# Three fill tiles per recurrence chunk, 116 fill units per attention head, and the second expert table without a loop

## The chip, the cores and the metric

The kernel runs on one core of a Trainium2 chip. The metric is device time in microseconds (us) of one execution, the median of three runs. A core has five engines that run side by side and wait for each other on semaphores: TensorE (PE; its weight loads are shown apart as PEld), VectorE (DVE), ScalarE (ACT), GpSimd (POOL) and SyncE (SP). SP, ACT and POOL also start DMA transfers. Each engine takes its instructions strictly in the order in which they were written.

## The reference

One step of a streaming encoder layer for 512 prompt and 32 sample positions (544 columns, width 2048), all in 32-bit floats:

```
h = rmsnorm(x); qkv|z|b|a|dq|dk|dv|gate_a|gate_b = split(h @ w_in)
o_a = gated_delta_rule(conv(qkv), ...)        # blocks of 64 positions, a state carried from block to block
o_b = (softmax1 - lam * softmax2) @ V          # 8 heads, block-causal
x += (sigmoid(gate_a)*(o_a @ w_a) + sigmoid(gate_b)*(o_b @ w_b)) @ w_out
x += cross_attend(rmsnorm(x), memory)
x += sum over 8x16 chosen experts of gate * gelu(xb . u[e]) * v[e]     # tables u, v: 16384 x 2048
y  = rmsnorm(x)
```

The expert layer is computed for 416 of the 544 columns by running all 16384 experts (gates of the experts not chosen are zero), and for the other 128 columns (the tail) by fetching the chosen rows of u and v.

## The kernel before

All large products are made from halves: a weight tile of 128x2048 is loaded into one of four ring slots, ACT rounds it (round_w, round_e: 128x2048), DVE subtracts the rounded part from the tile (split_w, split_e: 128x2048), and PE multiplies hi*hi, hi*lo and lo*hi. PE may begin tile n when the split of n is done, ACT may round tile n when PE has finished tile n-2, and SP may load it when PE has finished tile n-4. So every tile passes through ACT and DVE, in their order of instructions, while PE works on the tile before.

**Fill.** 56 tiles (projections of h for q, k, v and the two gates of the attention branch) are not computed in a stage of their own. They are cut in 32 units each, three matmuls of 272 columns per unit, and the function fill (L861) puts units into PE's stream between the small steps of two stages that are chains of PE, ACT and DVE: 9 chunks of the recurrence (128 units, four tiles, in each) and 8 heads of the attention (80 units in each). The tables GDN_FILL and ATT_FILL give the number of units ahead of each wait: d_a units ahead of the wait for DVE's d_a, a_x ahead of ACT's a_x, and so on. On ACT, serve (L1390) evicts each half tile (16 units), sends it out by DMA and after a full tile rounds the next but one. On DVE, split_w stands at fixed places of a chunk; in the attention, split_tiles (L1855) puts the split of the tile that begins at unit 32k behind the part q of the head in whose stretch unit 32k - 12 lies. In part 0 of each head but the first, head_norm (L1847) of the head before stands ahead of that split.

**Second table.** 128 tiles of v, 48 matmuls of 416 columns each, in 17 segments: 4 tiles, 15 times 8 tiles, 4 tiles. PE runs segments 1 to 14 as a hardware loop of seven passes of 16 tiles (L1263), the others are written out. At a segment's end DVE adds the eight PSUM banks into Y (sums). Per tile DVE also adds one fetched expert row block into the tail (tail_add, 128x2048). Once in 8 tiles two sets of coefficients (four experts' rows each) are loaded (load_quad on SP), multiplied (coefficients, on DVE), rounded (round_c, on ACT) and split (split_c, on DVE); the set for tiles 8B+2 and 8B+3 is needed two tiles after the first.

**Final norm.** ACT squares Y, PE sums the squares over 2048 rows with 64 matmuls against a matrix of ones, ACT takes the root, DVE the reciprocal, and 16 products give the result, which SP sends out in four parts.

Of the kernel before, what the change touches and what calls it, by code (L numbers as in the profile page):

```python
# [72 lines left out]

F_GDN = 4 * (NCH + 1)
W_BEFORE = W_MERGE + T_PQ - T_MERGE
# [32 lines left out]
def program(nc, t):  # L108
    with ExitStack() as ctx:
# [310 lines left out]
        def hi_of(n):  # L420
            return w_first[n % 2] if n < T_FILL else f_hi[n % 2] if n <= T_FILL + F_GDN else w_hi[n % 2]

# [93 lines left out]
        pick_v = [view(arena, KD * NT + b * D, 1, D)[0][:, 0, :] for b in range(4)]  # L516
        Y = H[:, :, :]
        Z = M
        e_in = [sem(f"e_in{b}") for b in range(R)]
# [27 lines left out]
        def _(sp):  # L547
# [26 lines left out]
            for tile in range(T_FILL + R, T_MERGE + R):  # L574
                c = (tile - R - T_FILL) // 4 + 1
                if (tile - R - T_FILL) % 4 == 0 and 2 <= c <= NCH:
# [201 lines left out]
        def _(pe):  # L778
# [457 lines left out]

            def pair_tiles(m0, begins, ends, seg, reg=None):

                for p in range(4):
                    n = E_V + m0 + p  # L1240
                    first, last = begins and p == 0, ends and p == 3
                    pe.wait_ge(w_split, upto(W_BEFORE + n + 1, reg, 16))
                    if m0 % 8 == 0 and p % 2 == 0:
                        pe.wait_ge(c_split, upto(m0 // 4 + p // 2 + 1, reg, 4))
                    for d in range(8):
                        if first:
                            pe.wait_ge(y_free, upto(8 * seg + d + 1, reg, 16))
# [30 lines left out]
            pe.wait_ge(y_free, 8 * N_BLOCKS + 16)  # L1278
            norm_pe(pe, "final", Z)


        @block.scalar
        def _(act):
# [366 lines left out]
            act.wait_ge(x_done, 3)  # L1650
            norm_act(act, "final", Y, Z)


        @block.vector
        def _(dve):
# [111 lines left out]
            def gdn_block(c, dyn):  # L1767
# [7 lines left out]
                if c:  # L1775
                    split_w(T_FILL + 4 * c + 1)
                dve.wait_ge(s["p_g"], one)
# [29 lines left out]
                    .then_inc(s["d_r"], 1)  # L1807
                split_w(T_FILL + 4 * c + 2)
                for lv in range(1, LEVELS):
# [6 lines left out]
                    if lv == 2:  # L1816
                        split_w(T_FILL + 4 * c + 3)
                dve.wait_ge(s["p_ks"], one)
# [379 lines left out]
            def sums(seg):  # L2198
                for d in range(8):
                    dst = Y[:, 8 * (seg % 2) + d, 0:ND]  # L2200
                    dve.wait_ge(y_full, 8 * seg + d + 1)
                    nc.vector.tensor_tensor(dst, dst, psum[:, d, 0:ND], ALU.add).then_inc(y_free, 1)

            for B in range(N_BLOCKS):
                more = B < N_BLOCKS - 1
                for half in range(2):
                    for p in range(4):
# [7 lines left out]
                        if m == 3:  # L2215
                            dve.wait_ge(x_moved, 48)
                        if m % 8 == 3 or m == 8 * N_BLOCKS - 1:
# [8 lines left out]
            dve.drain().then_inc(x_done, 1)  # L2226
            dve.wait_ge(root_ready, 5)
            nc.vector.reciprocal(root, root)
            dve.drain()
# [149 lines left out]
```

## Time and profile before

| | |
|---|---|
| three runs | 5408.36, 5415.87, 5424.44 us (median 5415.87) |
| profiled execution | 5427.89 us, its span from first to last instruction 5426.3 us |
| PE busy | 5176.1 us (95%), 36030 matmuls |
| DVE busy | 3011.2 us (55%) |
| ACT busy | 1616.1 us (30%) |
| POOL busy | 574.0 us (11%) |
| mean granted TensorE clock | 0.978 of full speed |

Times inside the profile count from the span's start. The recurrence lies at 660 to 1285, the attention at 1300 to 1706, the second table at 4091 to 5380 and the final norm at 5380 to 5426. A busy PE is not a PE at full pace: the duration of a matmul overlaps that of the next, and its pace is the distance from start to start. The granted clock of a stretch is 1.00 where TensorE had its 2.4 GHz all through, and lower where it ran some of the time at 1.2 GHz.

### The profile page before, as it was taken

How to read it: one execution, taken by the hardware profiler on the slowest of the kernel's cores; microseconds unless marked ns; L12 is line 12 of the kernel's file. 1: busy time of each engine (PE TensorE's matmuls, PEld its weight loads, DVE VectorE, ACT ScalarE, POOL GpSimd, SP SyncE). 2: the span in 40 equal slices, each digit the busy share in tenths (PEclk: the TensorE clock that was granted, in tenths of full speed). 3: DMA queues.
4: the chain of work that ended last, by engine and by line, in shares of the span. 5: the costliest groups of instructions: out<-in, count | busy, mean ns of one | idle time of the engine just before them, and what ended most of it. 6: DMA issues, size and time to landing. Idle time of an engine off the chain costs nothing.

```text
span 5426.3 us, 83831 instructions
## 1 busy us (share of the span) xinstructions
PE 5176.1 (95%) x36030; PEld 4981.6 (92%) x36030; DVE 3011.2 (55%) x4155; ACT 1616.1 (30%) x1765; POOL 574.0 (11%) x534
## 2 busy tenths in 40 slices
PE   7999999998888999999899999999999989999997
PEld 6999999997788999979899999999999989988897
DVE  5455544434555333222799788875545655655565
ACT  4434322223443222131222343432222222222222
POOL 0000000000000000000000122222211111111110
PEclk9999999999999999999999999999999999999999
DMA  6422332223223322222322588887767677777673
GB/s 229 153 101 99 109 92 83 90 88 104 88 99 121 131 94 83 89 86 86 125 102 102 209 313 306 311 309 278 277 227 288 245 254 248 245 256 245 239 270 138
DMA packets 257568, 951.58 MB, mean 175 GB/s; under 512 B 46464, under 2 KB 130560, under 8 KB 179456
## 3 DMA queue, kind: packets, MB, share of 16 engines
q1 hardware_dynamic: 181792, 552.11, 29.9%
q0 software_dynamic: 59360, 379.63, 18.4%
q10 hardware_dynamic: 16128, 15.60, 0.8%
q8 instruction: 228, 3.74, 0.3%
q14 instruction: 60, 0.49, 0.0%
HBM read 855.84 MB, written 91.43 MB: 175 GB/s over the span
## 4 chain that ended last, share of the span: by engine, by line
PE 78%; DVE 10%; issue 4%; DMA 2%; DVEq 2%; ACT 2%; PEld 1%; PEldq 0%; ACTq 0%; SPq 0%; POOL 0%; POOLq 0%
PE psum L1177 18%; PE psum L1252 16%; PE psum L1067 11%; PE psum L873 10%; PE psum L845 7%; PE psum L1084 4%; DVE e_lo L1984 2%; PE psum L821 2%; PE psum L1216 2%; PE psum L806 1%; DMA arena<-gates 1%; PEld psum L1252 1%; DVEq L2196 1%; DVE tmp L1883 1%; DMA ring<-in_v 1%
## 5 line engine op out<-in xcount | busy, mean ns | idle before, releaser
L1984 DVE TENSOR_TENSOR e_lo<-ring,e_hi 128x2048 fp32r<-128x2048 f32 x270 | 618.7, 2292 | 507.9 <-ACT e_hi L1495 491.6
L1495 ACT ACTIVATE e_hi<-ring 128x2048 fp32r<-128x2048 f32 x270 | 517.3, 1916 | 1009.1 <-PE psum L1252 851.2
L1252 PE MATMUL psum<-c_hi,e_hi 128*128 128x416 f32 x2048 | 733.9, 358 | 71.4 <-issue 36.2
L1252 PE MATMUL psum<-c_lo,e_hi 128*128 128x416 f32 x2048 | 727.4, 355 | 17.8 <-issue 17.8
L1252 PE MATMUL psum<-c_hi,e_lo 128*128 128x416 f32 x2048 | 731.5, 357 | 0.0
L1177 PE MATMUL psum<-h_hi,e_hi 128*128 128x416 f32 x2032 | 718.5, 354 | 5.5 <-DVE e_lo L1984 5.5
L1177 PE MATMUL psum<-h_hi,e_lo 128*128 128x416 f32 x2048 | 721.8, 352 | 0.0
L1177 PE MATMUL psum<-h_lo,e_hi 128*128 128x416 f32 x2032 | 710.4, 350 | 0.0
L873 PE MATMUL psum<-p_hi,e_lo 128*128 128x272 f32 x1792 | 525.0, 293 | 0.0
L1252 PEld LDWEIGHTS psum<-c_hi,e_hi 128*128 128x128 f32 x2048 | 392.4, 192 | 87.7 <-issue 63.7
L1252 PEld LDWEIGHTS psum<-c_lo,e_hi 128*128 128x128 f32 x2048 | 392.8, 192 | 27.2 <-issue 21.1
L1252 PEld LDWEIGHTS psum<-c_hi,e_lo 128*128 128x128 f32 x2048 | 392.2, 191 | 3.7
L1177 PEld LDWEIGHTS psum<-h_hi,e_hi 128*128 128x128 f32 x2032 | 381.5, 188 | 11.2 <-DVE e_lo L1984 7.7
L1177 PEld LDWEIGHTS psum<-h_lo,e_hi 128*128 128x128 f32 x2032 | 382.1, 188 | 5.4
L1177 PEld LDWEIGHTS psum<-h_hi,e_lo 128*128 128x128 f32 x2048 | 384.0, 188 | 3.1
L873 PE MATMUL psum<-p_hi,f_hi 128*128 128x272 f32 x1184 | 360.2, 304 | 0.7 <-ACT arena L1383 0.7
L873 PEld LDWEIGHTS psum<-p_hi,e_lo 128*128 128x128 f32 x1792 | 346.5, 193 | 0.0
L873 PE MATMUL psum<-p_lo,f_hi 128*128 128x272 f32 x1184 | 341.4, 288 | 0.0
L773 POOL DMA_INDIRECT arena<-in_v,eidx x128 | 221.7, 1732 | 1033.8 <-DVEq L2196 1007.4
L1580 ACT ACTIVATE tmp<-psum 128x416 f32<-128x416 f32 x128 | 66.3, 518 | 818.0 <-PE psum L1177 818.0
L2194 DVE SCALAR_TENSOR_TENSOR arena<-arena 128x2048 f32<-128x2048 f32 x127 | 297.9, 2345 | 0.0
L1297 ACT ACTIVATE w_hi<-ring 128x2048 fp32r<-128x2048 f32 x83 | 158.6, 1911 | 317.4 <-PE psum L1067 164.4
(433 smaller groups left out, 10227.1 us busy)
## 6 DMA issues: line engine op xcount, KB each, us to landing
ring<-in_weights SPq DMA_DIRECT2D x200, 1024.0 KB, 4.8
ring<-in_uT SPq DMA_DIRECT2D x128, 1024.0 KB, 5.1
ring<-in_v SPq DMA_DIRECT2D x128, 1024.0 KB, 7.0
hid<-tmp POOLq DMA_DIRECT2D x128, 208.0 KB, 6.2
gates<-arena POOLq DMA_DIRECT2D x13, 2048.0 KB, 10.0
arena<-hid SPq DMA_DIRECT2D x32, 832.0 KB, 10.5
arena<-gates SPq DMA_DIRECT2D x32, 832.0 KB, 13.9
gate_in<-tmp ACTq DMA_DIRECT2D x64, 136.0 KB, 2.9
```

Source lines behind the costliest of these rows:

```text
L773: pool.indirect_dma_start(pick_v[k % 4], None, experts, bass.IndirectOffsetOnAxis(eidx[:, k:k + 1], 0))\
L821: mm = nc.tensor.matmul(psum[:, 2 * (n % 2), 0:MEM], a, b[:, k, :], start=(k == 0 and j == 0), stop=(k == KD - 1 and j == 2))
L845: mm = nc.tensor.matmul(acc[j % 2][:, b, :], a, x[:, k, b * HN:(b + 1) * HN], start=(k == 0 and n == 0), stop=(k == KD - 1 and n == 2))
L873: mm = nc.tensor.matmul(psum[:, b, 0:HN], a, x[:, k, tok], start=(k == 0 and n == 0), stop=(k == KD - 1 and n == 2))
L1067: mm = nc.tensor.matmul(acc[j % 2][:, b, :], w, x[:, k, b * HN:(b + 1) * HN], start=(k == 0 and n == 0), stop=(k == KD - 1 and n == 2))
L1084: mm = nc.tensor.matmul(dst[:, b, :], a, x[:, k, b * HN:(b + 1) * HN], start=(k == 0 and n == 0), stop=(k == HEADS - 1 and n == 2))
L1177: mm = nc.tensor.matmul(psum[:, 2 + r % 2, 0:ND], w, h[:, c, 0:ND], start=(c == 0 and i == 0), stop=(c == KD - 1 and i == 2))
L1252: mm = nc.tensor.matmul(psum[:, d, 0:ND], w, c[p // 2][:, 2 * (p % 2) + r, :], start=(first and r == 0 and j == 0), stop=(last and r == 1 ...
L1297: nc.scalar.activation(hi_of(n), ring[:, tile % R, :], ACT.Copy).then_inc(w_rounded, 1)
L1495: nc.scalar.activation(hi_slot(n, reg), e_raw[n % R], ACT.Copy).then_inc(w_rounded, 1)
L1984: nc.vector.tensor_tensor(e_lo[n % R], e_raw[n % R], as_f32(hi_slot(n, reg)), ALU.subtract)\
L2194: add = nc.vector.scalar_tensor_tensor(out=ytok, in0=pick_v[k % 4], scalar=coef_t[:, k:k + 1], in1=ytok, op0=ALU.mult, op1=ALU.add)
```

## The change

Four things are edited. A chunk of the recurrence takes three tiles of the fill (96 units) and a head of the attention 116 units, with new tables of where the units stand; the fourth split_w of a chunk goes, and the others follow the new tile numbers. PE's loop over the second table is written out. In the second table, ACT rounds a set of coefficients ahead of the tile round that it stood behind, DVE makes both sets one tile later, and tail_add of the first two rows moves behind the splits of tiles 2 and 3. The final norm is taken apart: the 416 columns are squared row by row as they come out of the last two segments and added on DVE, so that one matmul is left for them, and the 128 tail columns follow with 16 matmuls of 128 columns.

```diff
-GDN_FILL = {"c_qb": 8, "c_kv": 16, "d_gu": 4, "d_a": 26, "d_r": (8, 7, 7, 7, 7), "a_x": 4, "d_rr": 9,
-            "a_vn": 5, "a_o": 4}
-ATT_FILL = {"vt": 6, "a": (10, 9, 11, 13, 13), "aT": (2, 2, 2, 5, 2), "obs": 5}
-GDN_UNITS, ATT_UNITS = 128, 80
+GDN_FILL = {"c_qb": 8, "c_kv": 20, "d_gu": 4, "d_a": 16, "d_r": (5, 5, 5, 5, 5), "a_x": 2, "d_rr": 6,
+            "a_vn": 4, "a_o": 3}
+ATT_FILL = {"vt": 12, "a": (14, 12, 14, 16, 17), "aT": (8, 4, 3, 6, 4), "obs": 6}
+F_CHUNK = 3
+GDN_UNITS, ATT_UNITS = F_CHUNK * F_TILE, 116
...
-                split_w(T_FILL + 4 * c + 4)
...
-            with pe.Fori(0, N_BLOCKS // 2 - 1) as i:
-                pair_tiles(4, True, False, 1, i)
-                pair_tiles(8, False, True, 1, i)
-                pair_tiles(12, True, False, 2, i)
-                pair_tiles(16, False, True, 2, i)
-            pair_tiles(8 * N_BLOCKS - 12, True, False, N_BLOCKS - 1)
-            pair_tiles(8 * N_BLOCKS - 8, False, True, N_BLOCKS - 1)
+            for seg in range(1, N_BLOCKS):
+                pair_tiles(8 * seg - 4, True, False, seg)
+                pair_tiles(8 * seg, False, True, seg)
...
-            norm_pe(pe, "final", Z)
+            pe.wait_ge(sq_added, SQ_DENSE + KD - 1)
+            nc.tensor.matmul(psum[:, 4, 0:ND], ones, dense_sq, start=True, stop=True).then_inc(ss_ready, 1)
+            for c in range(4):
+                pe.wait_ge(sq_tile, 3 * KD + c + 1)
+                for k in range(4):
+                    mm = nc.tensor.matmul(psum[:, 5, 0:TAIL], ones, tail_sq[:, 4 * c + k, :],
+                                          start=(c == 0 and k == 0), stop=(c == 3 and k == 3))
...
+            def dense_square(n):
+                act.wait_ge(x_tile, 2 * KD + n + 1)
+                if n >= 3:
+                    act.wait_ge(sq_added, SQ_DENSE + max(n - 3, 1))
+                nc.scalar.activation(dense_rows[n % 3], Y[:, last_order(n), 0:ND], ACT.Square).then_inc(sq_tile, 1)
...
-                    if n < E_END:
-                        round_e(n)
                     if B < N_BLOCKS - 1 and p == 6:
                         round_c(2 * B + 2)
                     if B and p == 0:
                         round_c(2 * B + 1)
+                    if n < E_END:
+                        round_e(n)
...
+                    if seg >= N_BLOCKS - 1:
+                        dve.drain().then_inc(x_tile, 1)
+                    if seg == N_BLOCKS and d:
+                        dense_add(KD // 2 + d - 1)
...
-                        tail_add(m)
-                        if more and (m % 8 == 3 or m % 8 == 4):
-                            coefficients(2 * B + 2 + (m % 8) // 4)
+                        if m < 8 * N_BLOCKS - 1:
+                            for k in tail_rows(m):
+                                tail_add(k)
+                        if more and (m % 8 == 4 or m % 8 == 5):
+                            coefficients(2 * B + 2 + m % 8 - 4)
```

On PE, at the end of a pass over 16 tiles of the second table, stood before (L1263 is the loop, c_hi, c_lo the coefficients' halves, e_hi, e_lo the tile's):

```order
L1252 MATMUL psum<-c_hi1_74,e_hi1_72 128x416
L1252 MATMUL psum<-c_lo1_76,e_hi1_72 128x416
L1252 MATMUL psum<-c_hi1_74,e_lo3_58 128x416
L1263 REGISTER_ALU
L1263 COMPARE_AND_BRANCH
```

and in the changed kernel at the same point, the next tile's first matmul directly behind:

```order
L1265 MATMUL psum<-c_lo1_76,e_hi1_72 128x416
L1265 MATMUL psum<-c_hi1_74,e_lo3_58 128x416
L1265 MATMUL psum<-c_hi0_73,e_hi0_71 128x416 [waits y_free,w_split]
L1265 MATMUL psum<-c_lo0_75,e_hi0_71 128x416
L1265 MATMUL psum<-c_hi0_73,e_lo0_55 128x416
```

The branch and its register step are gone; the matmuls and their order are the same.

On ACT, inside a block of 8 tiles of the second table, stood before (e_hi is a tile's rounded half, c_hi a set of coefficients):

```order
L1495 ACTIVATE e_hi1_72<-ring 128x2048 [waits e_end,e_in3]
L1495 ACTIVATE e_hi0_71<-ring 128x2048 [waits e_end,e_in0]
L1628 ACTIVATE c_hi0_73<-arena 128x1664 [waits e_end,c_ready]
L1495 ACTIVATE e_hi1_72<-ring 128x2048 [waits e_end,e_in1]
L1495 ACTIVATE e_hi0_71<-ring 128x2048 [waits e_end,e_in2]
L1628 ACTIVATE c_hi1_74<-arena 128x1664 [waits e_end,c_ready]
L1495 ACTIVATE e_hi1_72<-ring 128x2048 [waits e_end,e_in3]
```

and in the changed kernel:

```order
L1511 ACTIVATE e_hi1_72<-ring 128x2048 [waits e_end,e_in3]
L1644 ACTIVATE c_hi0_73<-arena 128x1664 [waits e_end,c_ready]
L1511 ACTIVATE e_hi0_71<-ring 128x2048 [waits e_end,e_in0]
L1511 ACTIVATE e_hi1_72<-ring 128x2048 [waits e_end,e_in1]
L1644 ACTIVATE c_hi1_74<-arena 128x1664 [waits e_end,c_ready]
L1511 ACTIVATE e_hi0_71<-ring 128x2048 [waits e_end,e_in2]
```

Each c_hi has moved ahead of one tile's round, whose wait is for one tile more of PE.

On DVE, in part 0 of the attention's third head (from the last product of the part to the next part's scores; L1850 and L1852 are head_norm), stood before:

```order
L1891 SCALAR_TENSOR_TENSOR H<-H,tmp 128x128
L1850 RECIPROCAL tmp<-tmp 128x544 [waits att_rt]
L1852 SCALAR_TENSOR_TENSOR arena<-tmp,lamb 128x544
L1872 SCALAR_TENSOR_TENSOR H<-H,const,psum 128x256 [waits att_s]
L1883 TENSOR_REDUCE tmp<-H 128x1
```

and in the changed kernel:

```order
L1926 SCALAR_TENSOR_TENSOR H<-H,tmp 128x128
L1885 RECIPROCAL tmp<-tmp 128x544 [waits att_rt]
L1887 SCALAR_TENSOR_TENSOR arena<-tmp,lamb 128x544
L1706 TENSOR_TENSOR e_lo3_58<-ring,w_hi1_60 128x2048 [waits w_rounded]
L1907 SCALAR_TENSOR_TENSOR H<-H,const,psum 128x256 [waits att_s]
```

A split now stands behind head_norm; before, part 0 of no head had one.

## Rows read from the trace of the kernel before

**Rows 1.** Busy time by stretch (start:end us, engines, granted clock, DMA share, GB/s).

```profile
4139.00:4288.00 149.00, 145.85 (x769) 143.18 (x768) 98.01 (x61) 36.59 (x20) 28.24 (x16) 1.00 0.78 272
4288.00:4454.00 166.00, 151.55 (x770) 147.60 (x768) 96.06 (x56) 36.57 (x20) 26.58 (x16) 0.95 0.70 244
4620.00:4781.00 161.00, 150.06 (x771) 146.06 (x769) 96.05 (x56) 36.59 (x20) 28.24 (x16) 0.97 0.72 252
946.00:1017.00 71.00, 71.00 (x856) 65.67 (x854) 29.96 (x43) 20.10 (x29) 0.00 (x0) 1.00 0.29 87
1300.00:1706.00 406.00, 364.61 (x2544) 328.67 (x2544) 211.78 (x370) 163.66 (x338) 19.09 (x36) 0.94 0.26 90
```

**Rows 2.** Waits, second table and final norm: total us, times, longest.

```profile
PE psum L1252 <- issue: 54.0, 21, 5.9
PE psum L1252 <- DVE e_lo L1984: 33.9, 20, 6.8
```

**Rows 3.** Waits, the loop's first pass alone (4139 to 4288).

```profile
PE psum L1252 <- issue: 0.3, 1, 0.3
```

**Rows 4.** Timeline of PE at the second jump back (start, duration, idle before).

```profile
4459.59 0.71 PE L1252 MATMUL psum<-c_hi,e_hi 128*128 128x416 f32 x1 [5.35 <-issue]
```

**Rows 5.** Timeline of DVE, second table, third pass.

```profile
4514.39 1.89 DVE L2171 TENSOR_TENSOR c_lo<-arena,c_hi 128x1664 fp32r<-128x1664 f32 x1 [8.26 <-ACT c_hi L1628]
4518.66 2.29 DVE L1984 TENSOR_TENSOR e_lo<-ring,e_hi 128x2048 fp32r<-128x2048 f32 x1
...
4557.53 1.89 DVE L2166 TENSOR_TENSOR arena<-arena 128x1664 f32<-128x1664 f32 x1 [8.62 <-DMA arena<-gates]
```

**Rows 6.** Timeline of DVE and ACT, beginning of the second table.

```profile
4114.25 1.29 DVE L2192 TENSOR_SCALAR arena<-arena 128x2048 f32<-128x2048 f32 x1 [17.32 <-DMA arena<-in_v,eidx]
4133.41 1.92 ACT L1495 ACTIVATE e_hi<-ring 128x2048 fp32r<-128x2048 f32 x1 [20.24 <-DMA ring<-in_v]
```

**Rows 7.** Chain that ended last (start, us, what): final norm, and fill in a chunk.

```profile
5389.64 16.61 PE psum L266 x64
946.12 10.01 PE psum L873 x78
```

**Rows 8.** Timeline of DVE, final norm.

```profile
5380.21 0.59 DVE L2202 TENSOR_TENSOR H<-H,psum 128x416 f32<-128x416 f32 x1 [0.55 <-PE psum L1252]
5407.01 3.55 DVE L2228 RECIPROCAL tmp<-tmp 128x544 f32<-128x544 f32 x1 [19.60 <-ACT tmp L200]
```

**Rows 9.** Timeline of DVE in one chunk of the recurrence.

```profile
946.21 0.16 DVE L1778 COPY tmp<-psum 128x4 f32<-128x4 f32 x1 [2.98 <-PE psum L922]
949.10 0.43 DVE L1787 TENSOR_TENSOR tmp<-tmp,const 128x256 f32<-128x256 f32 x1 [1.40 <-ACT tmp L1421]
950.93 0.42 DVE L1794 TENSOR_TENSOR tmp<-tmp,const 128x256 f32<-128x256 f32 x1
952.82 0.68 DVE L1800 TENSOR_TENSOR tmp<-H,tmp 128x512 f32<-128x512 f32 x1
956.79 0.42 DVE L1803 TENSOR_TENSOR tmp<-const,psum 128x256 f32<-128x256 f32 x1 [3.29 <-PE psum L929]
957.62 0.42 DVE L1806 TENSOR_TENSOR tmp<-tmp,const 128x256 f32<-128x256 f32 x1
```

**Rows 10.** Timeline of ACT at a chunk's end.

```profile
1001.17 0.40 ACT L1401 ACTIVATE tmp<-psum 128x272 f32<-128x272 f32 x1 [1.46 <-PE psum L873]
1003.98 1.28 ACT L1437 ACT_TABLE_LOAD   x1
```

**Rows 11.** Timeline of DVE in one head of the attention.

```profile
1452.51 0.35 DVE L1872 SCALAR_TENSOR_TENSOR H<-H,const,psum 128x128 f32<-128x128 f32 x1 [7.22 <-PE psum L1013]
1455.07 0.35 DVE L1891 SCALAR_TENSOR_TENSOR H<-H,tmp 128x128 f32<-128x128 f32 x1
1458.96 0.78 DVE L1852 SCALAR_TENSOR_TENSOR arena<-tmp,lamb 128x544 f32<-128x544 f32 x1
1472.65 2.28 DVE L1670 TENSOR_TENSOR e_lo<-ring,w_hi 128x2048 fp32r<-128x2048 f32 x1
```

More of the change, by code:

```diff
@@ L72 @@
 W_MERGE = T_MERGE
-F_GDN = 4 * (NCH + 1)
+F_GDN = F_CHUNK * (NCH + 1)
 W_BEFORE = W_MERGE + T_PQ - T_MERGE
@@ L517, in program, with last_order @@
         Y = H[:, :, :]
+        dense_rows = [view(arena, 3 * D + b * ND, 1, ND)[0][:, 0, :] for b in range(3)]
+        dense_sq = view(arena, 3 * D + 3 * ND, 1, ND)[0][:, 0, :]
+        tail_sq, e = view(arena, BIG + 4 * CQ, KD, TAIL)
+        assert 4 * ND <= D and e <= BIG + OAB_N
+        SQ_DENSE = 1 + 2 * (KD - 2)
+        flat_root = root.rearrange("p a b -> p (a b)")
+        def last_order(n):
+            return (n + KD // 2) % KD
         Z = M
@@ L574, in _ @@
             for tile in range(T_FILL + R, T_MERGE + R):
-                c = (tile - R - T_FILL) // 4 + 1
-                if (tile - R - T_FILL) % 4 == 0 and 2 <= c <= NCH:
+                c = (tile - R - T_FILL) // F_CHUNK + 1
+                if (tile - R - T_FILL) % F_CHUNK == 0 and 2 <= c <= NCH:
                     load_chunk(c)
@@ L1235, in _, with pair_tiles @@
             pe.sem_inc(y_free, 8)
-            def pair_tiles(m0, begins, ends, seg, reg=None):
+            def pair_tiles(m0, begins, ends, seg):
                 for p in range(4):
@@ L1278, in _ @@
             pe.wait_ge(y_free, 8 * N_BLOCKS + 16)
-            norm_pe(pe, "final", Z)
+            pe.wait_ge(sq_added, SQ_DENSE + KD - 1)
[5 more added lines that the diff above has]
+                                          start=(c == 0 and k == 0), stop=(c == 3 and k == 3))
+            mm.then_inc(ss_ready, 1)
         @block.scalar
@@ L1649, in _ @@
                         round_c(2 * B + 1)
-            act.wait_ge(x_done, 3)
-            norm_act(act, "final", Y, Z)
+                    if n < E_END:
+                        round_e(n)
+                    if n >= E_END - 2 and n < E_END:
+                        for k in range(4):
+                            dense_square(4 * (n - E_END + 2) + k)
+            for n in range(KD // 2, KD):
+                dense_square(n)
+            for c in range(4):
+                act.wait_ge(x_tile, 3 * KD + c + 1)
+                nc.scalar.activation(tail_sq[:, 4 * c:4 * c + 4, :], Y[:, 4 * c:4 * c + 4, ND:NT], ACT.Square)\
+                    .then_inc(sq_tile, 1)
+                if c == 1:
+                    act.wait_ge(ss_ready, SUMS["final"])
+                    nc.scalar.activation(flat_root[:, 0:ND], psum[:, 4, 0:ND], ACT.Sqrt, bias=eps, scale=1.0 / D)\
+                        .then_inc(root_ready, 1)
+            act.wait_ge(ss_ready, SUMS["final"] + 1)
+            nc.scalar.activation(flat_root[:, ND:NT], psum[:, 5, 0:TAIL], ACT.Sqrt, bias=eps, scale=1.0 / D)\
+                .then_inc(root_ready, 1)
         @block.vector
@@ L1775, in gdn_block @@
                 if c:
-                    split_w(T_FILL + 4 * c + 1)
+                    split_w(T_FILL + F_CHUNK * c + 1)
                 dve.wait_ge(s["p_g"], one)
@@ L1807, in gdn_block @@
                     .then_inc(s["d_r"], 1)
-                split_w(T_FILL + 4 * c + 2)
+                split_w(T_FILL + F_CHUNK * c + 2)
                 for lv in range(1, LEVELS):
@@ L1816, in gdn_block @@
                     if lv == 2:
-                        split_w(T_FILL + 4 * c + 3)
+                        split_w(T_FILL + F_CHUNK * c + 3)
                 dve.wait_ge(s["p_ks"], one)
@@ L2202, in sums, with dense_add, tail_rows @@
                     nc.vector.tensor_tensor(dst, dst, psum[:, d, 0:ND], ALU.add).then_inc(y_free, 1)
+                    if seg >= N_BLOCKS - 1:
+                        dve.drain().then_inc(x_tile, 1)
+                    if seg == N_BLOCKS and d:
+                        dense_add(KD // 2 + d - 1)
+                if seg == N_BLOCKS:
+                    dense_add(KD - 1)
+            def dense_add(n):
+                dve.wait_ge(sq_tile, 2 * KD + n + 1)
+                nc.vector.tensor_tensor(dense_sq, dense_rows[0] if n == 1 else dense_sq, dense_rows[n % 3], ALU.add)
+                dve.drain().then_inc(sq_added, 1)
+            def tail_rows(m):
+                if m < 2:
+                    return range(0)
+                return range(m - 2 + min(m - 2, 2), m - 1 + min(m - 1, 2))
             for B in range(N_BLOCKS):
@@ L2216, in _ @@
                             dve.wait_ge(x_moved, 48)
+                        if m >= 8 * N_BLOCKS - 3:
+                            for n in range(*((1, 4), (4, 7), (7, 8))[m - 8 * N_BLOCKS + 3]):
+                                dense_add(n)
+                        if m == 8 * N_BLOCKS - 1:
+                            tail_add(m)
                         if m % 8 == 3 or m == 8 * N_BLOCKS - 1:
                             sums((m + 1) // 8)
-                        tail_add(m)
-                        if more and (m % 8 == 3 or m % 8 == 4):
-                            coefficients(2 * B + 2 + (m % 8) // 4)
+                        if m < 8 * N_BLOCKS - 1:
[3 more added lines that the diff above has]
+                            coefficients(2 * B + 2 + m % 8 - 4)
             for c in range(4):
@@ L2225, in _ @@
                 nc.vector.tensor_tensor(dst, dst, psum[:, c, :].rearrange("p (k n) -> p k n", k=4), ALU.add)
-            dve.drain().then_inc(x_done, 1)
-            dve.wait_ge(root_ready, 5)
-            nc.vector.reciprocal(root, root)
+                dve.drain().then_inc(x_tile, 1)
+            for n, cols in enumerate((slice(0, ND), slice(ND, NT))):
+                dve.wait_ge(root_ready, 5 + n)
+                nc.vector.reciprocal(flat_root[:, cols], flat_root[:, cols])
             dve.drain()
```

8 lines of the change are left out of this document (4 added, 4 removed).

## The prediction

> **What bounds the kernel now.** I read the busy time by stretch first, then the waits of PE, then the timelines of DVE and ACT where a wait pointed. PE is the engine to follow: in a chunk of the recurrence it is busy for all of the 71 us and at full clock, and in the first pass over the second table for 146 of 149 us [rows 1]. Time is lost in three places. The later passes of the same loop take 166 or 161 us instead of 149, at a mean clock of 0.95 or 0.97 [rows 1]; most of PE's waiting there is put down to issue, which means that PE waited for nothing but its own instructions [rows 2]. In the first pass, the same instructions come straight from the code ahead, and issue costs 0.3 us [rows 3]; at a jump back PE stands for 5.35 us [rows 4]. Second, the attention: PE is busy for 364.6 of 406 us, clock 0.94 [rows 1]. Third, the end, where 46.1 us lie between the last sum of the table and the end of the span (5426.3 - 5380.2) [rows 8], 16.6 of them PE's norm sums [rows 7].
>
> **The second table.** Written out, seven passes should go as the first one does. Three later passes of 166 us and three of 161 us sum to 981; six of 149 are 894. That is 87 us, with the clock that falls at each jump and the late coefficients of three passes in it. What is late next is inside the first pass too: the waits of PE for the split of a tile, 33.9 us in 20 waits over the whole table [rows 2]. Fifteen of them, once per 8 tiles, come about so: ACT rounds the second set of coefficients only behind a tile round that waits for one PE tile more; DVE, next in its order, waits 8.26 us for it, then adds a tail row and only at 4518.66 begins the split that PE wants, done at 4520.95 [rows 5]. In the new order ACT rounds the set one tile (about 9.3 us, 149/16) sooner, which is more than the 8.26, so the wait goes. I price it at 1.2 us each, 18 us in all; the bounds are 0 and 27 (33.9 less its longest wait, 6.8, which is the one at the table's beginning). The second set's product is made one tile later. It waited 8.62 us for its load in a block where that stopped PE [rows 5]; 9.3 us later the load is there, and DVE (98 of 149 us busy [rows 1]) has room. What ACT moves ahead waits for an earlier PE tile than the round behind it, so nothing queued there is held up.
>
> At the table's beginning I expect no gain. DVE waited 17.3 us for the first gathered row with the split of tile 2 queued behind, and that goes; but the tile that opens segment 1 lands only at 4133.41, and with 1.92 and 2.29 us for round and split PE cannot pass it before 4137.6 [rows 6]. It passed it at 4139.5 before. PE now stands there for longer at once and resumes at 1.2 GHz: I take +1 us, between -2 and +5.
>
> **The end.** Nothing is added in front of PE's last tile but row squares on ACT and row additions on DVE (about 0.5 us each by the 0.59 of a 128x416 sum [rows 8]; ACT is busy for a quarter and DVE for two thirds of a pass [rows 1]). Counted from 5380.2: last sum and two row additions to 2.4; four tail additions of about 0.75 to 5.4, with PE's 416-column sum and ACT's root beside them, done at 6.5; tail squares, their 16 matmuls and root to 8.9; the dense reciprocal from 6.5 to 9.2 (2.7, by 3.55 x 416/544 [rows 8]), the tail's to 10.0. From the reciprocal's end to the span's end it was 15.7 us (5426.3 - 5410.6), which stays. 25.7 against 46.1: 20 us less, between 12 and 25.
>
> **The recurrence.** PE does 78 fill matmuls in 10.01 us [rows 7], 0.128 each and 0.385 a unit. 32 units fewer are 12.3 us a chunk, if nothing that they hid comes out. Three waits do:
> The tile end now falls on the last unit ahead of the decay step (8 + 20 + 4 = 32). There ACT evicts, sends and rounds before it loads its table: 1001.17 to 1003.98, and 1.28 more, 4.1 us [rows 10], instead of standing ready. PE's step (1.1) and DVE's first products end at 2.8, so ACT's exponentials start 1.3 late. DVE's d_a came 5.1 us after PE's step (946.21 to 951.35) [rows 9], now 6.4; PE has 16 units, 6.2, and with the signals waits 0.6.
> Then DVE does four more products, to 2.15 us behind d_a (953.50), and three for d_r, 1.25 (956.79 to 958.04) [rows 9]: 3.4. PE has 0.6 of its own step and five units, 2.5: a wait of 0.9.
> The second tile ends two units into the third d_r stretch. ACT is away for 2.8 us, then needs 0.4 for the copy that PE awaits; PE has three units, a step of 0.7 and two units, 2.6: a wait of 0.6.
> The others stay covered: d_r takes 1.2 against five units (1.9), the copies 0.5 against two units (0.8). So a chunk loses 12.3 - 2.1 = 10.2, nine of them 92 us; I add 5 us for stretches at 1.2 GHz, price unknown between 0 and 33 (below). With no wait at all it would be 111.
>
> **The attention.** It takes the 288 units, +111 us at full pace, and they cover most of the 41 us that PE stood. What stays or is new: PE's wait for the copy of the head's output, ahead of which no fill stands, about 1 us in each head; and the splits, which are placed by a margin of 12 units, 4.6 us, before their tile. In part 0 of a head DVE has the product ready 2.9 us after the scores (1452.51 to 1455.42), then head_norm until 1459.74, then 2.28 us of split: 9.5 us [rows 11]. In the third head the tile begins 12 units into that part: PE waits 4.9 us. In the sixth it begins at 16 units (14 and 2), a wait of 3.4. In part 2 a split began 4.5 us after the scores (1468.15) [rows 11]; by the growth from 2.9 I estimate 5.4 for part 3 and 6.0 for part 4. The fifth head's tile at 13 units of part 3 then waits 2.6, the seventh's at 15 units of part 4 2.4; smaller ones make 2. That is 15 us; ACT's rounds next to short stretches give 3 more, so 26 with the 8. The mean clock of 0.94 means some 49 of 406 us at half pace, which cost about 20 where PE had work; I keep 14 for the new waits, which are fewer and longer. Sum: 111 - 41 - 20 + 26 + 14 = +90, between +65 and +115.
>
> **Sum.** -87 - 18 + 1 - 20 - 92 + 5 + 90 = -121 us. The profiled execution took 5427.9 and lies 12.0 above the median of the runs (5415.9); the difference should hold for both, so 5307 for an execution like the profiled one and 5295 for the median.
>
> **Rivals.**
> A. The short waits in the recurrence bring TensorE down to 1.2 GHz as those in the attention did. For it: the attention's mean of 0.94 with waits of 1 to 2.5 us. Against it: the first pass of the table holds two waits of 1.2 us and has 1.00 [rows 1]. At 0.94 nine chunks of 61 us have 66 us at half pace, which is 33 us instead of my 5: 5323. The Trainium skill (TensorE: Matmul & The Clock Gate, A second HAM failure mode: psum-queue depth-cycling) says that brief idling between groups of matmuls is enough to make the clock swing between its levels; by it this rival would be the forecast, by the first pass it is not.
> B. The attention's splits come early enough, because PE is itself held up in front of them and the waits overlap: 25 us less, 5270.
> C. The second set of coefficients stays late, because the faster table asks more of the transfers. A pass with it takes 5 us more (166 against 161); in 14 blocks that is 70, in half of them 35: 5330. Against it: the first pass already moved 272 GB/s at a DMA share of 0.78 [rows 1], and the new pace is 2% above.
> D. The other side: instruction fetch. The straight code has 96 tiles' matmuls more to bring in beside full transfers. If a wait like that at the jump (5.35 us [rows 4]) came in 23 of these 96 tiles, all of the 121 us would be gone, and beyond that the kernel is slower; one in every second tile makes 5295 + 257 = 5552. Against it: 768 matmuls of the first pass with 0.3 us of issue. The Trainium skill (Runtime: NRT & Kernel Launch, Instruction fetch mechanics) has sequential fetch run ahead and mostly hidden, and a taken branch stop it; by it D would cost nothing, as in the first pass.
>
> **Chances.** Forecast 0.52 (5275 to 5315), A 0.15, B 0.20, C 0.09, D 0.04. The range of 5258 to 5340 takes in A, B and C and the open ends of clock and end. A measurement of this kernel can tell about 0.3%, 16 us, from no change. Faster by more than that 0.95, within it 0.01, slower 0.04.
>
> **What would show it.** In the profile of the changed kernel: no issue wait in the second table and passes of about 146 us for 16 tiles at clock 1.00; PE's waits for e_lo there gone but for the beginning; chunks of about 61 us with waits for DVE twice and ACT once; the attention at about 490 us, with PE waiting for e_lo, most of all in the third head; about 26 us from the last sum to the end. Passes still over 155 us would refute the largest term, an attention under 465 or over 515 us the least sure one.

## The result, and the profile after

The changed kernel takes 5288.94 us (median of four runs, 5286.91 to 5289.28), against 5420.15 for the kernel before in the same comparison: a ratio of 0.976, 95% interval 0.9743 to 0.9778, so 131 us faster. The forecast was 5295 us, with a range of 5258 to 5340. The profiled execution took 5289.28 us, its span is 5287.7.

The busy time by stretch of the changed kernel (columns as in [rows 1]): two passes of 16 tiles over the second table, one chunk of the recurrence, the attention.

```profile
4285.00:4431.00 146.00, 145.48 (x769) 143.49 (x768) 96.08 (x57) 36.60 (x20) 25.60 (x16) 1.00 0.79 277
4431.00:4577.00 146.00, 145.31 (x769) 143.33 (x768) 95.91 (x57) 36.60 (x20) 25.59 (x16) 1.00 0.79 277
727.40:788.50 61.10, 59.23 (x760) 53.77 (x759) 27.60 (x43) 17.39 (x26) 0.00 (x0) 1.00 0.28 80
1204.00:1688.00 484.00, 457.58 (x3408) 425.67 (x3408) 231.57 (x379) 187.51 (x364) 19.09 (x36) 0.98 0.29 100
```

A pass now takes 146 us at full clock (the first 148.6, below), where [rows 1] had 149, 161 and 166; a chunk 61 instead of 71; the attention 484 instead of 404 (the 406 of [rows 1] has rounded ends). PE's waits in the second table (total us, times, longest):

```profile
PE psum L1265 <- DVE H L2237: 9.9, 2, 9.7
PE psum L1265 <- issue: 3.9, 14, 0.4
```

The 54.0 us of issue and the 33.9 of waits for e_lo [rows 2] have become 3.9 and one stall at the table's beginning, which is 9.7 long. The profile puts it to DVE's sums; PE's weight load at the same place waits 10.0 us for e_lo, the split that the prediction named. The second set of coefficients, on DVE in the third pass (start, duration, idle before): its product, its split, and the tile split that PE wants.

```profile
4434.03 1.89 DVE L2201 TENSOR_TENSOR arena<-arena 128x1664 f32<-128x1664 f32 x1 [0.19 <-issue]
...
4456.49 2.29 DVE L2019 TENSOR_TENSOR e_lo<-ring,e_hi 128x2048 fp32r<-128x2048 f32 x1 [2.71 <-ACT e_hi L1511]
4458.70 1.89 DVE L2206 TENSOR_TENSOR c_lo<-arena,c_hi 128x1664 fp32r<-128x1664 f32 x1
```

Neither the load (8.62 us of waiting in [rows 5]) nor ACT's rounding (8.26) is waited for any more. PE's waits in nine chunks of the recurrence, and then in the attention:

```profile
PE psum L956 <- ACT tmp L1442: 5.1, 9, 0.8
PE psum L949 <- DVE tmp L1842: 4.8, 9, 0.5
PE psum L942 <- DVE tmp L1830: 4.7, 9, 0.5
```

```profile
PE psum L886 <- DVE e_lo L1706: 15.4, 7, 4.8
...
PE psum L1029 <- ACT tmp L1491: 7.6, 8, 2.2
PE psum L1037 <- DVE H L1926: 2.3, 3, 1.3
```

L942 is the wait for d_a, L949 for the first d_r, L956 for a_x of the third step; L886 is a fill tile's first unit, L1029 the scores of a head's part 4, L1037 the wait for a part's last products. Why d_a is late can be read in one chunk: ACT is still rounding a fill tile (f_hi) when the decay step begins, loads its table and makes the exponentials only then, and DVE waits for them.

```profile
721.26 1.92 ACT L1313 ACTIVATE f_hi<-ring 128x2048 fp32r<-128x2048 f32 x1 [0.46 <-ACT tmp L1417]
723.20 1.28 ACT L1434 ACT_TABLE_LOAD   x1
...
725.83 0.43 DVE L1823 TENSOR_TENSOR tmp<-tmp,const 128x256 f32<-128x256 f32 x1 [2.76 <-ACT tmp L1437]
```

In the attention the longest wait, 4.8 us, is in the third head: DVE is still in head_norm (the reciprocal and the product behind it) and starts the split late.

```profile
1330.63 0.35 DVE L1926 SCALAR_TENSOR_TENSOR H<-H,tmp 128x128 f32<-128x128 f32 x1
1330.90 3.54 DVE L1885 RECIPROCAL tmp<-tmp 128x544 f32<-128x544 f32 x1
1334.52 0.78 DVE L1887 SCALAR_TENSOR_TENSOR arena<-tmp,lamb 128x544 f32<-128x544 f32 x1
1335.23 2.28 DVE L1706 TENSOR_TENSOR e_lo<-ring,w_hi 128x2048 fp32r<-128x2048 f32 x1
```

And PE, at the same place:

```profile
1332.51 0.29 PE L886 MATMUL psum<-p_hi,e_lo 128*128 128x272 f32 x1
1337.56 0.59 PE L886 MATMUL psum<-p_hi,w_hi 128*128 128x272 f32 x1 [4.76 <-DVE e_lo L1706]
```

Last the end, on DVE (L2229 is a tail addition, L2237 a sum, L2247 the addition of a row's squares, L2288 the reciprocal of the 416 columns). PE's last matmul of the table ended at 5258.20.

```profile
5249.64 2.35 DVE L2229 SCALAR_TENSOR_TENSOR arena<-arena 128x2048 f32<-128x2048 f32 x1
5252.11 1.31 DVE L2237 TENSOR_TENSOR H<-H,psum 128x416 f32<-128x416 f32 x2
...
5260.02 0.59 DVE L2237 TENSOR_TENSOR H<-H,psum 128x416 f32<-128x416 f32 x1
5260.75 0.59 DVE L2247 TENSOR_TENSOR arena<-arena 128x416 f32<-128x416 f32 x1
5261.46 0.59 DVE L2237 TENSOR_TENSOR H<-H,psum 128x416 f32<-128x416 f32 x1
...
5267.75 2.75 DVE L2288 RECIPROCAL tmp<-tmp 128x416 f32<-128x416 f32 x1 [1.03 <-ACT tmp L1683]
```

The last sum starts 3.3 us behind PE, where it used to start at once [rows 8]. Of that 1.8 us are there at the first sum already: its bank was done at 5250.27, but DVE comes out of the row and tail additions that now stand ahead of the sums only at 5252. The other 1.4 come on the way, because a sum and an addition together take 1.44 us (5260.02 to 5261.46) and PE delivers a bank every 1.13.

### The profile page after: what moved, and what is told of

Same layout as the page of the kernel before. It is cut to its first block, busy times and chain, and to the rows that moved or that the text cites. A ratio compares the mean times of both kernels' runs of the same rounds, so it can differ in the third digit from the quotient of the medians.

```text
span 5287.7 us, 83626 instructions
## 1 busy us (share of the span) xinstructions
PE 5118.6 (97%) x36000; PEld 4943.1 (93%) x36000; DVE 3021.0 (57%) x4171; ACT 1619.9 (31%) x1782; POOL 555.1 (10%) x534
## 4 chain that ended last, share of the span: by engine, by line
PE 84%; DVE 9%; issue 2%; ACT 2%; DVEq 2%; DMA 1%; ACTq 0%; POOL 0%; SPq 0%; POOLq 0%; PEldq 0%
PE psum L1265 21%; PE psum L1190 19%; PE psum L1080 11%; PE psum L886 10%; PE psum L858 7%; PE psum L1097 4%; PE psum L834 2%; PE psum L1229 2%; PE psum L819 1%; DVE e_lo L2019 1%; DMA ring<-in_v 1%; ACT f_hi L1313 1%; PE psum L1114 1%; PE psum L1148 1%; DVE e_lo L1706 1%
## 5 line engine op out<-in xcount | busy, mean ns | idle before, releaser
L1265 PE MATMUL psum<-c_hi,e_hi 128*128 128x416 f32 x2048 | 719.9, 351 | 14.7 <-DVE H L2237 9.9
L1265 PE MATMUL psum<-c_lo,e_hi 128*128 128x416 f32 x2048 | 716.0, 350 | 0.0
L886 PE MATMUL psum<-p_hi,e_lo 128*128 128x272 f32 x1792 | 520.1, 290 | 0.0
L886 PEld LDWEIGHTS psum<-p_hi,e_lo 128*128 128x128 f32 x1792 | 341.4, 190 | 0.0
L786 POOL DMA_INDIRECT arena<-in_v,eidx x128 | 200.3, 1565 | 949.5 <-DVEq L2231 929.2
L2229 DVE SCALAR_TENSOR_TENSOR arena<-arena 128x2048 f32<-128x2048 f32 x127 | 298.0, 2346 | 1.4 <-DMA arena<-in_v,eidx 0.7
L886 PE MATMUL psum<-p_hi,w_hi 128*128 128x272 f32 x896 | 271.1, 303 | 15.5 <-DVE e_lo L1706 15.4
L886 PE MATMUL psum<-p_hi,f_hi 128*128 128x272 f32 x896 | 277.1, 309 | 0.7 <-ACT arena L1399 0.7
L1313 ACT ACTIVATE w_hi<-ring 128x2048 fp32r<-128x2048 f32 x92 | 175.9, 1912 | 322.5 <-PE psum L1080 164.8
```

Source lines behind the costliest of these rows:

```text
L786: pool.indirect_dma_start(pick_v[k % 4], None, experts, bass.IndirectOffsetOnAxis(eidx[:, k:k + 1], 0))\
L886: mm = nc.tensor.matmul(psum[:, b, 0:HN], a, x[:, k, tok], start=(k == 0 and n == 0), stop=(k == KD - 1 and n == 2))
L1313: nc.scalar.activation(hi_of(n), ring[:, tile % R, :], ACT.Copy).then_inc(w_rounded, 1)
L2229: add = nc.vector.scalar_tensor_tensor(out=ytok, in0=pick_v[k % 4], scalar=coef_t[:, k:k + 1], in1=ytok, op0=ALU.mult, op1=ALU.add)
```

## The experiments

Stage lengths below are read from PE's first and last matmul of the stage in each profile. Ratios are taken against the kernel before, run beside each set on the same chip; its median was 5429.34 us (23 runs, 5399.52 to 5442.35) beside the first four kernels, 5422.55 beside the next four and 5422.39 beside the last three. The changed kernel was not run beside the first eight; where a difference from it is given for them, it is from the 5288.94 us above. Its nine runs, in that set and beside the last three, lie between 5286.91 and 5290.98 us.

### The four parts, each alone on the kernel before

**The loop written out.**

```diff
...
-            with pe.Fori(0, N_BLOCKS // 2 - 1) as i:
-                pair_tiles(4, True, False, 1, i)
...
+            for seg in range(1, N_BLOCKS):
+                pair_tiles(8 * seg - 4, True, False, seg)
+                pair_tiles(8 * seg, False, True, seg)
```

> The kernel before with PE's loop over the second table written out and nothing else. Theory (the jumps back cost most of the table's gain): no issue wait over 1 us in the table, all seven passes at 149 us as the first one was, PE still waits some 25 to 34 us for the splits of tiles behind late coefficients; 87 us less than the kernel before, about 5333 us. Rival (three of the six slow passes were slow for another reason, their coefficients late by 3.8, 3.8 and 2.4 us with the clock fallen behind them): those waits stay, 72 us less, about 5348.

Measured: 5333.88 us, ratio 0.9833 (0.9816 to 0.9849). The table goes from 1287.4 to 1201.4 us. One pass and the waits over the whole table:

```profile
4438.00:4587.00 149.00, 146.31 (x769) 143.18 (x768) 95.86 (x57) 36.60 (x20) 30.23 (x16) 1.00 0.77 272
```

```profile
PE psum L1252 <- DVE e_lo L1980: 24.2, 18, 7.2
PE psum L1252 <- issue: 4.2, 16, 0.3
```

All passes are at 149 us, also those that took 166: none of the waits of 2.4 to 3.8 us for late coefficients is left without the loop. The 86.0 us are the forecast's 87. The runs gain 95.5, and in this trace the attention, which was not edited, is 10.5 us shorter than in the kernel before (last section).

**The order in the second table.**

```diff
-                    if n < E_END:
-                        round_e(n)
...
+                    if n < E_END:
+                        round_e(n)
...
-                        tail_add(m)
-                        if more and (m % 8 == 3 or m % 8 == 4):
-                            coefficients(2 * B + 2 + (m % 8) // 4)
+                        for k in tail_rows(m):
+                            tail_add(k)
+                        if more and (m % 8 == 4 or m % 8 == 5):
+                            coefficients(2 * B + 2 + m % 8 - 4)
```

> The kernel before with the new order of coefficients, rounds and tail additions alone; the loop over the second table stays. Theory (15 waits of 1.2 us come from the second set's rounding behind a tile round): PE's 33.9 us of waits for e_lo fall to the one at the table's beginning, about 7; the six waits at the jumps stay. 18 us less, or up to 33 if the three late sets of 5 us go too: 5387 to 5402. Rival (at the jumps PE gives ACT and DVE time to catch up, so that the order matters less while the loop stands): under 10 us less, over 5410.

Measured: 5389.11 us, ratio 0.9925 (0.9911 to 0.9939), table 1250.2 us: 37.2 less, a little more than the forecast's upper end of 33. The 15 waits for splits behind coefficients are gone; the six stalls at the jumps are as long as before (5.69 to 6.28 us from matmul to matmul, against 5.70 to 6.26), and passes take 158 us. This trace also warns of how such lines are read. The stall at the second jump:

```profile
4451.14 0.71 PE L1252 MATMUL psum<-c_hi,e_hi 128*128 128x416 f32 x1 [5.46 <-DVE e_lo L1984]
```

It is put to DVE because a split happens to end 0.16 us earlier. That split is of a tile later: the split of the tile that PE begins here ended at 4440.95. In [rows 4] the same stall is put to issue.

**The fill tables** (with the tile numbers that hang on them).

```diff
...
-GDN_UNITS, ATT_UNITS = 128, 80
...
+F_CHUNK = 3
+GDN_UNITS, ATT_UNITS = F_CHUNK * F_TILE, 116
```

> The kernel before with the new fill tables alone (three tiles a chunk, 116 units a head). Theory (the stages do not touch each other): chunks of 61 us with three waits of 0.5 to 0.6 us, attention of 484 us, both as in the changed kernel; 16.5 us less than the kernel before, about 5403. Rival (the later stages meet another state of rings and queues): the same two stages, but the sum differs by more than 5 us, because the merge or the tables begin otherwise.

Measured: 5416.80 us, ratio 0.9982 (0.9970 to 0.9993), 12.5 us less. The forecast's 16.5 lie 4 us off. The two stages are nearly those of the changed kernel (480.8 us for the attention, where that had 484.0):

```profile
731.00:792.00 61.00, 59.12 (x759) 53.64 (x758) 27.46 (x43) 17.39 (x26) 0.00 (x0) 1.00 0.27 80
1205.50:1686.30 480.80, 454.41 (x3408) 423.19 (x3408) 231.51 (x379) 187.51 (x364) 19.09 (x36) 0.98 0.29 100
```

**The final norm.**

```diff
-            norm_pe(pe, "final", Z)
+            nc.tensor.matmul(psum[:, 4, 0:ND], ones, dense_sq, start=True, stop=True).then_inc(ss_ready, 1)
...
+                    if seg == N_BLOCKS and d:
+                        dense_add(KD // 2 + d - 1)
```

> The kernel before with the new final norm alone. Theory of the prediction: from the table's last matmul to the end 25.7 us instead of 46.1, 20 us less, 5400. Theory from the changed kernel's trace (the eight sums of the last segment each have a row addition behind them on DVE, 1.43 us a pair against 1.13 us a bank on PE, so that the last sum comes 3 us behind PE): 29.5 us, 16.6 less, 5403.5.

Measured: 5419.91 us, ratio 0.9989 (0.9974 to 1.0004), 9.4 us less: not told apart from no change by the whole time. In the trace the end takes 29.3 us instead of 46.1, so the stage does gain 16.8. In its profiled execution the table, in passes that the edit does not reach, is 3.7 us longer than in the kernel before and the attention, not edited either, 4.3 longer. The same looped table took 1278.4 us in the run with the new fill tables, 1287.4 and 1291.1 in these two, so such differences come from one execution to the next. Where the other runs lose the rest is not shown.

**Do they add up?** The four medians give 95.5 + 40.2 + 12.5 + 9.4 = 157.6 us. In the table, the loop and the order save 86.0 and 37.2 alone and 106.2 together (1287.4 to 1181.2), so 17.0 are counted twice; about 15 of them are the three passes with late sets of coefficients (166 us for 161), which either edit brings down. The remaining 140.6 agree with 5429.3 - 5288.9 = 140.4, but not to the tenth: against the kernel before of its own set the changed kernel gained 131.2, against that of the last set 133.3, and the sum of the four holds unedited stages that varied by 10 us.

### What makes a jump back dear

The first table's last loop jumps back 12 times over 4 tiles, in the kernel before as in the changed one, and PE waits for nothing there but once for a split. In the kernel before, PE's only wait from 3622 to 4050 (us in all, times, longest):

```profile
PE psum L1177 <- DVE e_lo L1984: 0.3, 1, 0.3
```

So a jump alone is not the price. In the second table of the kernel before, each of the six jumps has two pauses: the one of [rows 4], 5.35 us, and one at the next matmul.

```profile
4464.94 0.72 PE L1252 MATMUL psum<-c_lo,e_hi 128*128 128x416 f32 x1 [2.56 <-issue]
```

Two variants of the changed kernel ask whether the length of the body decides.

```diff
...
-            for seg in range(1, N_BLOCKS):
-                pair_tiles(8 * seg - 4, True, False, seg)
-                pair_tiles(8 * seg, False, True, seg)
+            with pe.Fori(0, N_BLOCKS - 1) as i:
+                pair_tiles(4, True, False, 1, i)
+                pair_tiles(8, False, True, 1, i)
```

> The changed kernel with PE's second table as a loop again, but with a body of 8 tiles and 15 iterations, 14 jumps back (before: 16 tiles, 6 jumps). Theory 1 (a jump back costs, whatever it jumps over): 12 us a jump, the 69 us by which the six jumps of the kernel with the new order alone exceed the changed kernel's table; 14 of them are 161 us, table 1342 us, 5450 us in all. Theory 2 (the length of the body decides: the first table has jumps back over 8 and over 4 tiles, and no wait above 0.9 us at one of them): no stall, table 1181 us, 5289 us in all.

Measured: 5296.09 us, ratio 0.9769 (0.9753 to 0.9785): 7 us above the changed kernel, not 161. The table takes 1186.3 us instead of 1181.2: 16 tiles take 147.1 us instead of 146.1, so a jump costs 0.5, and the longest wait behind the table's beginning is 0.8:

```profile
PE psum L1265 <- DVE H L2237: 11.1, 15, 0.8
```

The queues that carry instructions tell the two loops apart (queue, packets, MB, share). First the kernel before over its last six passes of the loop, then the loop of 8 tiles over 1000 us of the table:

```profile
q8 instruction: 52, 0.85, 0.3%
q14 instruction: 9, 0.07, 0.0%
```

```profile
q14 instruction: 9, 0.07, 0.0%
```

On q8 the 16-tile body brings in about 9 packets of 16 KB in each pass, the 8-tile body none at all; q14 brings the same 9 with either, and in the straight code, which has 42 on q8 in the same 1000 us. At the jump of [rows 4] one packet of q8 arrives inside each of the two pauses, and PE goes on 1.3 to 1.7 us behind it. So the pauses are waits for instructions. The Trainium skill (Runtime: NRT & Kernel Launch, Instruction fetch mechanics) has a taken branch fetch its target anew whenever it is outside a window of two pages of 256 instructions. The runs differ here: 8 tiles are 768 matmuls and weight loads, more than two such pages, and 14 jumps over them fetched nothing on q8.

```diff
-            with pe.Fori(0, (NKEY - ROW_D) // 4) as i:
-                for q in range(4):
-                    row_tile(ROW_D + q + 16, ROW_D + q, i, 4, 4)
+            with pe.Fori(0, (NKEY - ROW_D) // 16) as i:
+                for q in range(16):
+                    row_tile(ROW_D + q + 16, ROW_D + q, i, 16, 16)
+            for r in range(NKEY - (NKEY - ROW_D) % 16, NKEY):
+                row_tile(r + 16, r)
```

> The changed kernel with PE's last loop over the first table, 13 passes of 4 tiles, taken as 3 passes of 16 tiles and 4 tiles written out: two jumps back over 16 tiles instead of twelve over 4. Theory 2 (the length of the body decides): two stalls of 5.4 to 6 us with 1.2 GHz behind them, 23 us more, first table 1491 us instead of 1468, 5312 us in all. Theory 3 (a jump is dear in the second table only, for what else goes on there): no stall, 1468 us, 5289 us.

Measured: 5295.29 us, ratio 0.9765 (0.9749 to 0.9782), 6 us more; the first table takes 1475.5 us instead of 1468.1. Neither theory fits. Of the two jumps, the first, at 3752, stalls nowhere, and no packet arrives on q8 in the second pass; at the second two packets of q8 arrive while PE stands:

```profile
3902.52 0.71 PE L1190 MATMUL psum<-h_hi,e_hi 128*128 128x416 f32 x1 [3.94 <-issue]
```

So in all these loops PE stood at a jump where code came in again on q8, and not where none did. A 16-tile body can go either way, so its length does not decide alone whether the code is fetched. What does is open.

### The new waits

**The splits in the attention.**

```diff
-                    if UNITS_AT[QT * h + q] <= F_TILE * k - 12 < UNITS_AT[QT * h + q + 1]:
+                    if UNITS_AT[QT * h + q] <= F_TILE * k - 20 < UNITS_AT[QT * h + q + 1]:
```

> The changed kernel with the attention's splits placed by a margin of 20 units instead of 12. Theory (12 units, 4.6 us, are too few for the products and the split of 2.3 us on DVE): PE's 15.4 us of waits for e_lo go, and with them 17 us at 1.2 GHz behind them, which cost half: 24 us less, attention 460 us instead of 484, 5265 us in all. Rival (DVE is the bound there, and an earlier split only makes its products late): PE waits for DVE's H or ACT's copies instead, attention above 476.

Measured: 5267.69 us, ratio 0.9718 (0.9701 to 0.9734), 21 us less than the changed kernel; attention 460.4 us, forecast 460. The waits for e_lo are gone; those at L1029 and L1037 stay as they were:

```profile
PE psum L1029 <- ACT tmp L1491: 7.6, 8, 2.2
PE psum L1037 <- DVE H L1926: 2.3, 3, 1.3
PE psum L1048 <- ACT tmp L1481: 2.2, 2, 1.9
```

**The tile's end in a chunk.**

```diff
-GDN_FILL = {"c_qb": 8, "c_kv": 20, "d_gu": 4, "d_a": 16, "d_r": (5, 5, 5, 5, 5), "a_x": 2, "d_rr": 6,
+GDN_FILL = {"c_qb": 8, "c_kv": 17, "d_gu": 4, "d_a": 16, "d_r": (5, 8, 5, 5, 5), "a_x": 2, "d_rr": 6,
```

> The changed kernel with three units of fill moved in each chunk from ahead of the K products (c_kv 17 instead of 20) to the second step of the recursion (d_r 8 instead of 5). The tile then ends three units into the d_a stretch, which keeps its 16 units, as the first d_r stretch its 5. Theory of the prediction (ACT's eviction and round at the tile's end make its exponentials late): the waits for d_a and for the first d_r go, 9.5 us less, 5279 us; the wait for a_x in the third step, 0.57, stays. Rival (16 and 5 units are too few for DVE, whatever ACT does): both waits stay at 0.5, 5289 us.

Measured: 5278.54 us, ratio 0.9733 (0.9717 to 0.9749), 10.4 us less. With the same 16 and 5 units ahead of them, the waits for d_a and the first d_r are gone, and a chunk takes 59.6 us instead of 60.8. Of the three lines one is left:

```profile
PE psum L956 <- ACT tmp L1442: 5.1, 9, 0.8
```

So the two waits came from ACT's work at the tile's end, and not from a stretch too short for DVE.

**The copy of the head's output.** The changed kernel ran once more beside the next two.

> The changed kernel once more, beside the two that follow on the same chip, so that differences of 7 us can be told: 5289 us within 3.

Measured: 5289.06 us, ratio 0.9745 (0.9728 to 0.9762).

```diff
+                    if q == 4:
+                        u = fill(u, ATT_FILL["o4"])
...
-ATT_FILL = {"vt": 12, "a": (14, 12, 14, 16, 17), "aT": (8, 4, 3, 6, 4), "obs": 6}
+ATT_FILL = {"vt": 12, "a": (14, 12, 14, 16, 14), "aT": (8, 4, 3, 6, 4), "o4": 3, "obs": 6}
```

> The changed kernel with three of the 17 units ahead of the last products of a head (part 4) put in front of that part's scores, so that PE has 1.15 us of fill while ACT copies the head's output. Theory (PE's wait there, 1.05 us in each of 8 heads and 2.45 in one, has nothing in front of it): seven of the 7.6 us of waits go, the 14 units left still cover DVE's products but for a part of 1 us in all; attention 477 us, 5282 us in all. Rival (part 4 then comes short: its products take DVE longer, and PE waits for H instead): no change, 5289.

Measured: 5288.48 us, ratio 0.9743 (0.9725 to 0.9760): no change. The attention takes 483.0 us. The waits for the copy fell from 7.6 to 1.1 us, and came back elsewhere (L1042 is the last wait of part 4):

```profile
PE psum L887 <- DVE e_lo L1710: 17.4, 8, 4.8
...
PE psum L1042 <- DVE H L1930: 3.7, 7, 0.6
PE psum L1040 <- DVE H L1930: 2.3, 3, 1.3
PE psum L1032 <- ACT tmp L1494: 1.1, 1, 1.1
```

The rival was right in the main: the 17 units of part 4 were needed where they stood.

**All of it**, with a recurrence table in which the second tile ends with the second step.

```diff
-GDN_FILL = {"c_qb": 8, "c_kv": 20, "d_gu": 4, "d_a": 16, "d_r": (5, 5, 5, 5, 5), "a_x": 2, "d_rr": 6,
+GDN_FILL = {"c_qb": 8, "c_kv": 16, "d_gu": 4, "d_a": 22, "d_r": (5, 5, 5, 4, 4), "a_x": 2, "d_rr": 6,
...
```

> The changed kernel with the margin of 20, the three units ahead of the last scores, and a recurrence table that takes four units from ahead of the K products and one each from the last two steps and gives six to the d_a stretch (c_kv 16, d_a 22, d_r 5, 5, 5, 4, 4), so that the first tile ends four units into d_a and the second with the second step. Theory (all three waits of a chunk go, 1.62 us; the attention loses its split waits, 24, and the copies, 7): chunks of 59.4 us, attention 453 us, 5244 us in all. Rival (what is taken from the other stretches comes out there: K products, later steps): a gain of only the attention's part, 5258.

Measured: 5248.36 us, ratio 0.9671 (0.9654 to 0.9688), 40.7 us less than the changed kernel beside it; this is the fastest version. A chunk in its window, PE busy throughout:

```profile
727.00:786.40 59.40, 59.40 (x763) 54.05 (x763) 27.93 (x43) 17.39 (x26) 0.00 (x0) 1.00 0.28 82
```

From chunk to chunk it is 59.0 us (60.8 in the changed kernel), all three waits gone. The attention took 458 us, not 453: PE waits 1.1 us in all for the copy, but 4.1 in 8 times at L1042, as when the three units were moved alone.

## Why the prediction was right

**The table, right in both its terms.** The loop: 87 forecast, 86.0 measured alone. The late splits and the beginning: 18 less 1 forecast, 20.2 measured (1201.4 to 1181.2 us). At the beginning PE passed the tile that opens segment 1 at 46.2 us after the table's start, against 46.7; it stands there once and for longer, as forecast, and the 1.2 GHz behind the stall now falls into the first pass, which takes 148.6 instead of 146.1 us. That is 2 us lost for the 1 forecast.

**The recurrence, its mechanism right, the exact number luck.** From chunk to chunk 71.02 us became 60.82, the 10.2 of the forecast. The three waits are the three that were named, and the run with the tile's end moved shows for the first two that the cause was the one given; the third went in the last kernel, where the second tile ends elsewhere. But they are 0.52, 0.53 and 0.57 us for 0.6, 0.9 and 0.6, which makes 1.6 for 2.1, and the 32 units were worth 11.8 (10.2 + 1.6) and not 12.3. The two misses cancel. The 5 us for the clock were not needed: it stayed at 1.00. Rival A falls with that. The Trainium skill (TensorE: Matmul & The Clock Gate, A second HAM failure mode: psum-queue depth-cycling) has brief idling make the clock swing; the trace does not show it here, where 27 waits of 0.5 to 0.8 us, three in a chunk, left it at 1.00. 4.7 us more came from ahead of the first chunk's end and from the gap before the attention (14.9 to 12.8 us), for which the sum had no term.

**The attention, its mechanism right, its size 10 us off.** +90 forecast, +80.0 measured (404.0 to 484.0). The waits are 26.2 us in all (15.4 + 7.6 + 2.3 + 0.9), the forecast's 26. The four that were forecast one by one, in the third, sixth, fifth and seventh heads, are 4.8, 3.9, 2.6 and 2.2 for 4.9, 3.4, 2.6 and 2.4. The mis-sized terms: 288 units took 0.377 us each and not 0.385, 2.4 less (from start to start a matmul takes 0.126 us; the prediction took 0.128 from [rows 7]), and TensorE ran at 1.2 GHz for 20 us behind the new waits, not 28, 4 less; the other 3.6 have no row. Rival B's 25 us were there to be had, but with another placement of the splits: the run with a margin of 20 made the attention 23.6 us shorter.

**The end, 3.4 us short.** 16.6 us gained (46.1 to 29.5) for 20. From the last sum to the end it is 26.2 us, 25.7 forecast. The step that failed is "last sum and two row additions to 2.4", counted from a last sum right behind PE. The additions that stand ahead of the eight sums and between them had no term; they put the last sum 3.3 us behind PE (1.8 ahead, 1.4 between).

**Rivals C and D** did not happen: every pass behind the first is at 146 us, issue costs 3.9 us in 14 waits over the whole table, and q8 brought 42 packets of instructions in 1000 us of it with no issue wait above 0.4.

**The sum, closer than its terms.** The profiled executions differ by 138.6 us (5427.89 to 5289.28); 121 were forecast. The attention (10), the clock and the entry of the recurrence (9.7), the splits (3) account for more than the difference, the end (3.4), the loop (1) and the stages between (0.8) go the other way. The step "the difference should hold for both" was wrong too: the profile of before lay 12 us above the median of its three runs, the one of after within 0.4. So 5307 for the profiled execution was 18 us too high and 5295 for the median only 6, because the 12 us that were taken off made up for most of the stages' miss. That part is luck.

## What to carry to other kernels

Before a hardware loop is written out, look whether instructions arrive in its passes at all: here a body of 16 tiles fetched its code again at six jumps, at 12 us each with the slow clock behind, and one of 8 tiles cost 5 to 7 us in all. When work that hid waits is cut, walk every stretch with the durations of the trace: the three waits of a chunk and the four long ones of the attention were found so. Ask at each what the engine that PE waits for did just before; in a chunk ACT was busy with the end of a tile, and moving that end took the wait away without one more unit of cover. Units moved to cover one wait are taken from another; count the cover they leave.

## What was not expected of the hardware

The same code and the same waits gave attentions of 393.5 us (the kernel with the loop written out) and 408.3 us (the one with the new norm), at a mean granted clock of 0.98 and 0.93; the kernel before had 404.0 and 0.94 [rows 1].

```profile
1302.00:1696.00 394.00, 352.95 (x2544) 316.50 (x2544) 211.80 (x370) 162.48 (x337) 19.08 (x36) 0.98 0.26 92
```

```profile
1298.00:1706.00 408.00, 368.53 (x2543) 332.00 (x2544) 211.77 (x370) 162.34 (x337) 19.08 (x36) 0.93 0.26 89
```

PE's waits differ by 1.4 us in all between the two (40.8 and 39.4, more in the faster one); what differs is the time at 1.2 GHz, 18 us against 56. The four waits of 2.3 us in this attention had a stretch at 1.2 GHz behind them three times in the kernel before and not once in the one with the loop written out, so the length of a wait does not tell alone. A stage with many waits can thus differ by 15 us between executions by the clock, and one trace of it is no exact base: the +80 above would have been +90 or +76 against these. The changed kernel's nine runs lie within 4.1 us of each other, 23 of the kernel before within 43. With the loop alone written out five runs still spread over 23 us, with the new fill tables alone eleven over 27.
